# Moving the third mixer's implicit filter and its transform to the start of a one-core, three-block Trainium2 kernel

## Chip, cores and metric

The kernel is one launch on one core of a Trainium2 chip. The metric is device time in microseconds (us) of that core; the time before is the median of 3 runs.

## What is computed

A two-layer diffusion-style block runs over 256 latent and 256 context rows of width 1024. A third block follows on 16 meta tokens and the 256 latent rows. Its mixer has a long convolution whose filter does not depend on the data that flows through the kernel: it comes from three small weight matrices, two sines and a decay. Cut to what matters here:

```python
def hyena_filter(L, w1, b1, w2, b2, w3, b3, freq):          # L = 272, D_HY = 512
    z = concatenate([t, cos(bands * w), -sin(bands * w)])    # constants, (272, 33)
    hdn = sin(freq[0] * (z @ w1 + b1))                       # (272, 64)
    hdn = sin(freq[1] * (hdn @ w2 + b2))
    k = (hdn @ w3 + b3).reshape(L, 2, D_HY) * exp(-t * deltas)
    return concatenate([k_fwd, zeros, k_bwd[:0:-1]])

def fft_long_conv(u, k_full, skip):                          # y = irfft(rfft(u) * rfft(k_full))[:L] + u * skip

def second_block(x, meta, ...):                              # the third mixer
    proj = rmsnorm(h) @ w_in
    y_hy = hyena_branch(proj[..., :s_hy], ...)               # short conv, fft_long_conv, projection
    y_rg = rglru_branch(...)                                 # two directions of conv, gates, scan
    merged = sigmoid(gates) * y_hy + sigmoid(gates) * y_rg
```

## The kernel before

All engines have their instructions written out by hand; the order on each queue is the order of the text. SyncE streams weight blocks of 512 KB into a ring of six places; a place is loaded again when its last block has begun (for unsplit blocks) or has been split. Most weight blocks are split by ScalarE (`high`, line 1575) and VectorE (`low`, line 1969) into a high and a low part, and TensorE does three products for each of eight chunks of 128 inputs.

The stages that matter here:

- **Start.** TensorE takes 16 modulation blocks `ada0a` (line 728). Behind block 7 stands `norm(0)`, the sum of squares of the input rows (line 767), behind block 11 the spread of the factor (line 782). `first_turn` (line 752) turns the modulation; ScalarE (line 1493) and VectorE make the split input chunk by chunk; the first projection tile of `ev_in` (line 939) takes each chunk as it comes, and nine tiles follow, the last five with a 128x512 product for the squares of queries and keys (line 834). Meanwhile VectorE has a chain of small steps at the very start (`softplus`, lines 1962 to 1969).
- **`fourier`.** Before its first product (line 819) TensorE takes eight modulation blocks.
- **Third mixer.** `mix` (line 1134) makes 44 projection tiles. Among them, on TensorE: `rg_gates(0)` and `rg_gates(1)` (line 1077), two small products for the filter's hidden layers (lines 1184 and 1187), six tap products (line 1195), and, between tiles 37 and 38, the filter's transform (`filter_dft`, line 1090: 18 fp32 products into five groups). VectorE makes the sine arguments (seven steps each), multiplies the taps by the decay (`filt`) and adds and subtracts them, between the `low` parts and the steps of the recurrent branch (`rg_conv`, `rg_logs`, `rg_ratio`, `rg_scan`). ScalarE does the two sines (with their table loads), the copies of the transform (`dft_copy`, line 1734) and the recurrent branch's functions; `mults(1)` (line 1726, a square root of 128x2176) stands behind three of the copies.
- On VectorE the three parts of `rg_scan(1, ...)` (lines 2301, 1969, 2308) stand ahead of `low_mix(40)`, so TensorE's tile 40 needs the scan.
- The filter's weights, the decay (1536 KB) and the transform's table (960 KB) are loaded by GpSimd just before the third mixer.

Of the kernel before, what the change touches and what calls it, by code (L numbers as in the profile page):

```python
# [14 lines left out]
F32 = mybir.dt.float32  # L15
F32R = mybir.dt.float32r
# [109 lines left out]
for _n, _c in PARAMS:  # L126
# [19 lines left out]
MASKO0 = 41984  # L146
# [6 lines left out]
PARTA0, PARTB0, PARTC0 = 30608, 38144, 42496  # L153
SQB0 = 14144
XC0, RG0, IG0, TG0, HFW0 = (14144 + 2176 * _i for _i in range(5))
FILT0 = 25024
HID0 = 26448
KF0 = 27536
KS0 = 32768
FCOS0 = 35840  # L160
# [13 lines left out]
RGATE0 = 25024  # L174
MT0 = 14144
# [19 lines left out]
SMALLS = [("ident", 128), ("ones", 128), ("block", 128), ("perm", 128), ("iota", 128), ("iota16", 16),  # L195
          ("pick", 12), ("strip", 4), ("eps", 1)]
# [55 lines left out]
def build(nc, t, out):  # L252
    with ExitStack() as ctx:
# [48 lines left out]
        with nc.sbuf_tensor("mixer_rows_place", [P, NP0], F32):  # L302
            with nc.sbuf_tensor("n0_parts", [P, 2 * DC * LT], F32R) as n0_parts:
                with nc.sbuf_tensor("mixer_gates_place", [P, PARTA0 - NP0 - 2 * DC * LT], F32):
                    with nc.sbuf_tensor("mix_w_parts0", [P, 2048], F32R) as mix_w_parts0:
                        with nc.sbuf_tensor("filter_place", [P, PARTB0 - PARTA0 - 2048], F32):
                            with nc.sbuf_tensor("mix_w_parts2", [P, 2048], F32R) as mix_w_parts2:
                                with nc.sbuf_tensor("residual_rows_place", [P, PARTC0 - PARTB0 - 2048], F32):
                                    with nc.sbuf_tensor("mix_w_parts1", [P, 2048], F32R) as mix_w_parts1:
                                        pass  # L310
# [13 lines left out]
        query_parts = {name: [[first, query_w_parts1, mix_w_parts1][(r - turn) % PARTS][:, :].rearrange("p (h n) -> p h n", h=2)  # L324
                              for r in range(PARTS)] for name, first in (("wq", query_w_parts0), ("peer0", ahead_w_parts0))}
        n0p = n0_parts[:, :].rearrange("p (h c n) -> p h c n", h=2, c=DC)
# [50 lines left out]
        ident, ones, block64, perm, iota = (small(n) for n in ("ident", "ones", "block", "perm", "iota"))  # L377

# [7 lines left out]
        hyena_in = sem("hyena_tables_in")  # L386
# [55 lines left out]
        pool_chain = sem("pool_chain")  # L442
        hres_ready = sem("second_residual_ready")
# [14 lines left out]
        bias_row = sem("filter_bias_row_ready")  # L458
# [3 lines left out]
        filt_sums = sem("filter_sums_ready")  # L462
# [120 lines left out]
        mask_o = view(MASKO0, QT, L)  # L583
# [82 lines left out]
        def _(pe):  # L666
# [118 lines left out]

            def fourier():
# [3 lines left out]
                for f in fill[0][:8]:  # L790
                    ada(*f)
                pe.wait_ge(even_in, 16 * 4)
# [266 lines left out]
            z = view(FILT0, LT, parts=EMB)  # L1059
            w1 = view(FILT0 + LT, HF, parts=EMB)  # L1060
            w2 = view(FILT0 + LT + HF, HF, parts=HF)
            w3 = view(FILT0 + LT + 2 * HF, 2 * HY, parts=HF + 1)
            hid = view(HID0, 4, LT)
            ktab, ks = view(FCOS0, 3, GW), view(KS0, 2, 3, HY)

# [15 lines left out]

            def filter_dft(g):

                if g >= 2:
                    pe.wait_ge(dft_copied, g - 1)
                o = bank[4 + g % 2]
                runs = [(0, P, g // 2)] if g < 4 else [(0, 64, 0), (64, P, 1)]
                for tt in range(3):
                    for lo, hi, src in runs:
                        mm = pe.matmul(o[lo:hi, :], ktab[0:TTW[tt], tt, g * P + lo:g * P + hi],  # L1090
                                       ks[0:TTW[tt], src, tt, :], start=(tt == 0), stop=(tt == 2))
                mm.then_inc(dft_ready, 1)
# [17 lines left out]
            def mix_first():  # L1110

                wb = [split_block(ORD["w_in2a"] + j, None, mwp) for j in range(2)]
                o = [bank_of(TILE["w_in2a"] + j) for j in range(2)]
                for k in range(DC):
                    pe.wait_ge(normed, DC * 4 + k + 1)
                    for j in range(2):
                        for n, (hw, hx) in enumerate(TERMS):
                            mm = pe.matmul(o[j][:, 0:LT], wb[j][:, hw, k, :], n0p[:, hx, k, :],
# [64 lines left out]
            pe.wait_ge(hyena_in, 16 * 6)  # L1183
            pe.matmul(bank[3][0:HF, 0:LT], w1, z, start=True, stop=True).then_inc(hid_ready, 1)
            mix(16, 24)
            pe.wait_ge(hid_sin, 1)
            pe.matmul(bank[4][0:HF, 0:LT], w2, hid[0:HF, 0, :], start=True, stop=True).then_inc(hid_ready, 1)
            mix(24, 28)
            pe.wait_ge(hid_sin, 2)
            pe.wait_ge(bias_row, 1)  # L1190
            for n in range(6):
                tt = n // 2
                if n >= 2:
                    pe.wait_ge(filt_read, n - 1)
# [6 lines left out]
            for g in range(GROUPS):  # L1201
                filter_dft(g)
# [1889 lines left out]
```

## Time and profile before

| | |
|---|---|
| median of 3 runs | 2191.51 us (2190.57 to 2192.89) |
| the profiled execution's own time | 2190.52 us |
| its span, first to last instruction | 2188.6 us |
| TensorE busy | 96% of the span |
| VectorE, ScalarE, GpSimd busy | 65%, 44%, 14% |
| mean granted TensorE clock | 0.988 |

The timeline has one row for a run of equal instructions: start and length in us, engine, line, operation, tiles written and read, count, and in brackets the idle time before it with what ended it. An fp32 product shows as two records of TensorE. PEld is TensorE's weight load. The page has shares by engine; the windows give busy time of each engine and the granted clock in a stretch.

### The profile page before, as it was taken

How to read it: one execution, taken by the hardware profiler on the slowest of the kernel's cores; microseconds unless marked ns; L12 is line 12 of the kernel's file. 1: busy time of each engine (PE TensorE's matmuls, PEld its weight loads, DVE VectorE, ACT ScalarE, POOL GpSimd, SP SyncE). 2: the span in 40 equal slices, each digit the busy share in tenths (PEclk: the TensorE clock that was granted, in tenths of full speed). 3: DMA queues.
4: the chain of work that ended last, by engine and by line, in shares of the span. 5: the costliest groups of instructions: out<-in, count | busy, mean ns of one | idle time of the engine just before them, and what ended most of it. 6: DMA issues, size and time to landing. Idle time of an engine off the chain costs nothing.

```text
span 2188.6 us, 35310 instructions
## 1 busy us (share of the span) xinstructions
PE 2102.2 (96%) x12873; PEld 1777.8 (81%) x12873; DVE 1432.7 (65%) x2494; ACT 972.8 (44%) x1532; POOL 315.3 (14%) x336
## 2 busy tenths in 40 slices
PE   6999999999989998999999999999999999999998
PEld 2745788888878747999998788999988888888886
DVE  4436544443258585665569776997996677777776
ACT  3335322222244365444476725546753444444444
POOL 0014000000013030000000004787840000000000
PEclk8999999999999999999999999999999999999999
DMA  8266222222235264455644434452146555555553
GB/s 319 78 228 244 87 96 96 96 96 96 96 93 162 87 248 167 164 182 184 208 157 143 171 122 155 165 183 78 68 144 221 180 195 190 187 188 191 188 188 124
DMA packets 92847, 342.90 MB, mean 157 GB/s; under 512 B 10393, under 2 KB 10420, under 8 KB 92224
## 3 DMA queue, kind: packets, MB, share of 16 engines
q1 hardware_dynamic: 89280, 325.10, 43.9%
q0 software_dynamic: 3456, 16.26, 2.4%
q8 instruction: 76, 1.25, 0.2%
q14 instruction: 35, 0.29, 0.0%
HBM read 340.27 MB, written 1.05 MB: 156 GB/s over the span
## 4 chain that ended last, share of the span: by engine, by line
PE 60%; issue 27%; DVE 8%; ACT 3%; DMA 2%; POOL 0%; SPq 0%; DVEq 0%; ACTq 0%; POOLq 0%
PE banks L939 20%; PE banks L986 8%; PE banks L1281 6%; PE banks L1134 3%; PE banks L1330 3%; PE banks L864 2%; PE banks L1314 2%; PE banks L1018 2%; DVE main_zone L1966 2%; PE banks L1403 1%; PE banks L728 1%; PE banks L890 1%; PE banks L953 1%; PE banks L911 1%; DVE main_zone L1969 1%
## 5 line engine op out<-in xcount | busy, mean ns | idle before, releaser
L939 PE MATMUL banks<-act_parts,first_w_parts 128*128 128x512 f32 (+1 forms) x2592 | 477.5, 345 | 6.0 <-DVE act_parts L1969 3.9
L939 PEld LDWEIGHTS banks<-act_parts,first_w_parts 128*128 128x128 f32 x2592 | 410.8, 190 | 69.6 <-issue 7.6
L1969 DVE TENSOR_TENSOR first_w_parts<-weight_ring,first_w_parts 128x1024 fp32r<-128x1024 f32 x166 | 206.8, 1248 | 258.6 <-ACT first_w_parts L1575 258.6
L1403 PE MATMUL banks<-w_parts,a_parts 128*128 128x512 f32 x1524 | 360.1, 390 | 0.6 <-DVE a_parts L1969 0.6
L1403 PEld LDWEIGHTS banks<-w_parts,a_parts 128*128 128x128 f32 x1524 | 285.9, 188 | 59.6 <-DVE a_parts L1969 1.0
L1969 DVE TENSOR_TENSOR w_parts<-weight_ring,w_parts 128x1024 fp32r<-128x1024 f32 x207 | 254.4, 1230 | 72.1 <-ACT w_parts L1575 72.0
L1575 ACT ACTIVATE w_parts<-weight_ring 128x1024 fp32r<-128x1024 f32 x207 | 218.9, 1058 | 184.2 <-PE banks L1369 102.0
L1575 ACT ACTIVATE first_w_parts<-weight_ring 128x1024 fp32r<-128x1024 f32 x166 | 174.7, 1057 | 232.5 <-PE banks L939 120.6
L1369 PE MATMUL banks<-n_parts,w_parts 128*128 128x512 f32 x632 | 229.4, 397 | 1.3 <-DVE w_parts L1969 1.3
L986 PE MATMUL banks<-ffn_hidden_parts,first_w_parts 128*128 128x512 f32 (+1 forms) x1056 | 183.4, 336 | 0.0
L986 PEld LDWEIGHTS banks<-ffn_hidden_parts,first_w_parts 128*128 128x128 f32 x1056 | 162.5, 190 | 20.6
L1372 PE MATMUL banks<-n_parts,w_parts 128*128 128x256 f32 x632 | 164.4, 281 | 0.0
L1369 PEld LDWEIGHTS banks<-n_parts,w_parts 128*128 128x128 f32 x632 | 118.6, 188 | 26.8 <-DVE w_parts L1969 1.7
L1134 PEld LDWEIGHTS banks<-n_parts,mix_w_parts 128*128 128x128 f32 x1008 | 123.7, 188 | 11.9 <-DVE mix_w_parts L1969 8.8
L1134 PE MATMUL banks<-n_parts,mix_w_parts 128*128 128x256 f32 (+1 forms) x1008 | 127.9, 287 | 5.2 <-DVE mix_w_parts L1969 5.2
L1969 DVE TENSOR_TENSOR banks<-banks,main_zone 128x256 f32<-128x256 f32 (+1 forms) x174 | 97.7, 566 | 53.2 <-ACT main_zone L1893 52.5
L1372 PEld LDWEIGHTS banks<-n_parts,w_parts 128*128 128x128 f32 x632 | 119.5, 189 | 6.1
L1969 DVE TENSOR_TENSOR mix_w_parts<-weight_ring,mix_w_parts 128x1024 fp32r<-128x1024 f32 x60 | 72.9, 1222 | 33.9 <-ACT mix_w_parts L1575 33.3
L1575 ACT ACTIVATE mix_w_parts<-weight_ring 128x1024 fp32r<-128x1024 f32 x77 | 81.0, 1053 | 16.4 <-PE banks L1134 7.9
L1893 ACT ACTIVATE main_zone<-banks 128x256 f32<-128x256 f32 x79 | 30.3, 384 | 124.3 <-PE banks L1369 124.3
L728 PE MATMUL banks<-weight_ring,small_zone 128*32 128x512 f32 x384 | 62.4, 641 | 18.6 <-DMA weight_ring<-in_stream 10.0
L2902 POOL DMA_DIRECT2D main_zone<-in_g_final x1 | 0.6, 616 | 538.9 <-DVE a_parts L1969 538.9
(296 smaller groups left out, 3055.8 us busy)
## 6 DMA issues: line engine op xcount, KB each, us to landing
weight_ring<-in_stream SPq DMA_DIRECT2D x618, 512.0 KB, 3.8
main_zone<-in_rel_bias POOLq DMA_DIRECT2D x6, 512.0 KB, 12.3
rounded<-in_dft_input POOLq DMA_DIRECT2D x1, 1600.0 KB, 7.0
main_zone<-in_decay POOLq DMA_DIRECT2D x1, 1536.0 KB, 9.4
rounded<-in_dft_inverse POOLq DMA_DIRECT2D x1, 1280.0 KB, 6.2
main_zone<-in_xT POOLq DMA_DIRECT2D x1, 1024.0 KB, 11.6
main_zone<-in_ctxT POOLq DMA_DIRECT2D x1, 1024.0 KB, 16.1
tail_zone<-in_rel_bias POOLq DMA_DIRECT2D x2, 512.0 KB, 24.1
```

The costliest lines, as they stand in the source:

```text
L728: mm = pe.matmul(bank[ADA_BANKS[phase][half]][strip:strip + 32, :], cond[:, k, 10 - 2 * row:42 - 2 * row], wb[:, half * 512:(half + 1) * 512],
L864: mm = pe.matmul(bank[b][:, :], fin[:, hx, c, tt * P:(tt + 1) * P], wb[:, hw, kk, :], start=(c == 0 and n == 0), stop=(c == DC - 1 and n = ...
L939: mm = pe.matmul(o[:, 0:w], wb[:, hw, k, :], fin[:, hx, k, 0:w], start=(k == 0 and n == 0), stop=(k == DC - 1 and n == 2))
L986: mm = pe.matmul(o[:, 0:w], wb[:, hw, b % 8, :], fhid[:, hx, k, 0:w], start=(k == 0 and n == 0), stop=(k == FC - 1 and n == 2))
L1134: mm = pe.matmul(o[:, cols], wb[:, hw, k, :], n0p[:, hx, k, cols], start=(k == 0 and n == 0), stop=(k == DC - 1 and n == 2))
L1281: mm = pe.matmul(o[:, 0:L], wb[:, hw, k, :], rows[:, hx, k, :], start=(k == 0 and n == 0), stop=(k == DC - 1 and n == 2))
L1330: mm = pe.matmul(twins[h][:, j * P:(j + 1) * P], one1[:, 8 * h + j, :], one2[:, 8 * h + j, :], start=True, stop=True)
L1369: return pe.matmul(o[:, :], w[:, 0, k, :], n2p[:, :, k, :], start=(k == 0), stop=(k == DC - 1))
L1372: return pe.matmul(o[:, 0:L], w[:, 1, k, :], n2p[:, 0, k, :], start=False, stop=False)
L1403: mm = pe.matmul(acc[n][:, :], ap_[:, e % 3, ha, (n // 2) * P:(n // 2 + 1) * P], wp[(B + b) % PARTS][:, hw, (n % 2) * 512:(n % 2 + 1) * 51 ...
L1575: act.activation(parts[n % PARTS][:, 0, :], slot(s), ACT.Copy).then_inc(w_hi, 1)
L1969: return dve.tensor_tensor(o, a, b, op)
```

## The change

The filter is made at the start. The first small product stands behind modulation block 2, the second behind block 4; the tap products 0 and 1 behind block 7, ahead of `norm(0)`; the others behind blocks 8 to 11. The sum and the difference of the two halves of the last weight matrix are made by VectorE before the products, so that the taps need no sums afterwards; GpSimd mends the first tap. The decay is made by ScalarE with 12 exponentials instead of being loaded. Of the transform, groups 0, 1 and 2 (nine products) go into and behind the first `ev_in` tile, groups 3 and 4 among the eight modulation blocks ahead of `fourier`. ScalarE copies the spectrum at these places (`dft_copy(0)` stands ahead of the last chunk of the split input). The spectrum stays in columns that are free until the third mixer; GpSimd moves the last group once. On the loads: the filter's first weights come ahead of the input rows, its last weights behind them, the transform's table when modulation block 14 begins, the rest of the small constants behind it, and the tables of `fourier` only after the first tile. The places of two split buffers move, the first block of the third mixer is split into another buffer, and the odd mask is 64 columns wide.

The core of the diff:

```diff
-SMALLS = [("ident", 128), ("ones", 128), ("block", 128), ...
+SMALLS = [("ones", 128), ("iota", 128), ("pick", 12), ("strip", 4), ("eps", 1), ("fade", 15),
+          ("ident", 128), ("block", 128), ("perm", 128), ("iota16", 16)]
+NEARLY = 288
...
+            def tap_product(n):
+                tt, src = n // 2, n % 2
+                if n == 0:
+                    pe.wait_ge(hid_sin, 2)
+                    pe.wait_ge(taps_w, 1)
+                if n >= 2:
+                    pe.wait_ge(filt_read, n - 1)
+                pe.matmul(bank[2 + n % 2][0:TTW[tt], :], hid[0:HF + 1, 2, tt * P:tt * P + TTW[tt]], w3_both[:, src, :],
+                          start=True, stop=True).then_inc(filt_ready, 1)
+            def filter_dft(g, steps=range(3)):
+                if 0 in steps:
+                    if g == 0:
+                        pe.wait_ge(ktab_in, 16)
+                        pe.wait_ge(filt_read, 6)
+                        pe.wait_ge(filt_fixed, 2)
+                    if g >= 2:
+                        pe.wait_ge(dft_copied, [1, 3, 4][g - 2])
...
+            def first_tile():
...
+                    if k >= 1:
+                        filter_dft((k - 1) // 3, [(k - 1) % 3])
+                filter_dft(2, [1, 2])
             def fourier():
-                for f in fill[0][:8]:
+                pe.wait_ge(dft_copied, 2)
+                for f in fill[0][:6]:
                     ada(*f)
+                filter_dft(3)
+                ada(*fill[0][6])
+                filter_dft(4)
+                ada(*fill[0][7])
+                pe.wait_ge(dft_copied, GROUPS)
...
             for b in range(16):
                 ada(0, "ada0a", b, b // DC, b // DC == 0, b // DC == 1)
+                if b in (2, 4):
+                    hidden(b // 2 - 1)
                 if b == 7:
+                    tap_product(0)
+                    tap_product(1)
                     norm(0)
+                if 8 <= b < 12:
+                    tap_product(b - 6)
                 if b == 11:
                     spread_rstd(0)
             first_turn()
-            for j in range(10):
-                split_tile("ev_in", j, T, k_norm=0 if j == 0 else None)
+            first_tile()
+            pe.wait_ge(tables_in, 16)
+            for j in range(1, 10):
+                split_tile("ev_in", j, T)
...
             rg_gates(0)
-            pe.wait_ge(hyena_in, 16 * 6)
...
+            mix(16, 34)
             rg_gates(1)
             mix(34, 38)
-            pe.wait_ge(filt_sums, 1)
-            for g in range(GROUPS):
-                filter_dft(g)
             mix(38, 44)
...
 ScalarE:
                 for c in range(DC):
+                    if k == 0 and c == DC - 1:
+                        dft_copy(0)
...
+            for tt in range(3):
+                for b in range(4):
+                    act.activation(decay[:, tt, b * P:(b + 1) * P], iota, ACT.Exp, ...
+            sine(0)
+            sine(1)
             norm(0)
...
             decays(1, lambda: split2(36, 38))
-            for g in range(3):
-                dft_copy(g)
             mults(1)
-            for g in range(3, GROUPS):
-                dft_copy(g)
...
 VectorE:
-            softplus()
+            softplus(0)
+            sine_arg(0)
+            dve.memset(hid[HF:HF + 1, 2, :], 1.0)
+            sine_arg(1)
+            softplus(1)
+            dve.wait_ge(taps_w_in, 16)
+            tt_(w3_both[:, 0, :], w3[:, 0, :], w3[:, 1, :], ALU.add)
+            tt_(w3_both[:, 1, :], w3[:, 0, :], w3[:, 1, :], ALU.subtract).then_inc(taps_w, 1)
+            filt(0)
+            filt(1)
             first_norm()
...
 GpSimd:
+            pool.dma_start(view(HYZ0, LT + 2 * HF, parts=HF), t["hyena_first"][:, :]).then_inc(hidden_in, 16)
             pool.dma_start(X[:, :, 0:L], ...
             pool.dma_start(X[:, :, L:T], ...
+            pool.dma_start(view(HYW0, 2 * HY, parts=HF + 1), t["hy_w3"][:, :]).then_inc(taps_w_in, 16)
...
+            pool.wait_ge(blocks_used, 15)
+            pool.dma_start(ktab, t["dft_filter"].rearrange("p (a n) -> p a n", a=3)).then_inc(ktab_in, 16)
             pool.wait_ge(ada_rows, 1)
+            pool.dma_start(view(SMALL0 + NEARLY, NSM - NEARLY), t["smalls"][:, NEARLY:NSM]).then_inc(tables_in, 16)
+            pool.wait_ge(tile_ready, TILE["ev_in"] + 1)
             pool.dma_start(view(DFTE0, 1280), t["dft_even"][:, :]).then_inc(even_in, 16)
```

How the instructions move, at the three places on which the prediction rests. First TensorE from its first modulation block on, before the change (small_zone holds constants, main_zone the input rows and work):

```order
L728 MATMUL banks<-weight_ring,small_zone 32x512 x16
L767 MATMUL banks<-main_zone,small_zone 32x128 x32
L728 MATMUL banks<-weight_ring,small_zone 32x512 x8
L782 MATMUL banks<-small_zone 128x128 x4
L728 MATMUL banks<-weight_ring,small_zone 32x512 x8
```

The same place now (L801 and L804 are the two hidden products, L814 the taps, L778 the sum of squares):

```order
L739 MATMUL banks<-weight_ring,small_zone 32x512 x6
L801 MATMUL banks<-main_zone 64x272
L739 MATMUL banks<-weight_ring,small_zone 32x512 x4
L804 MATMUL banks<-main_zone 64x272
L739 MATMUL banks<-weight_ring,small_zone 32x512 x6
L814 MATMUL banks<-main_zone 128x512 x2
L778 MATMUL banks<-main_zone,small_zone 32x128 x32
```

Four filter products now stand ahead of the sum of squares on TensorE.

Second, the end of the first `ev_in` tile on TensorE now (L842 are the tile's products, L830 the transform's, L1011 the next tiles):

```order
L842 MATMUL banks<-act_parts,first_w_parts 128x512 x3
L830 MATMUL banks<-tail_zone,main_zone 128x512
L842 MATMUL banks<-act_parts,first_w_parts 128x512 x3
L830 MATMUL banks<-main_zone 128x512
L830 MATMUL banks<-tail_zone,main_zone 128x512 x2
L1011 MATMUL banks<-act_parts,first_w_parts 128x512 x120
```

Before, the tile's 24 products and the next tiles' 120 were one unbroken run of 144 (L939).

Third, ScalarE in the third mixer behind the second direction's gates, before the change (L1720 and L1722 are the decay's exponential and square, L1734 the copies of the transform, L1726 the square root, L1575 the split of block 40):

```order
L1720 ACT_TABLE_LOAD
L1720 ACTIVATE main_zone<-main_zone 128x2176
L1722 ACTIVATE main_zone<-main_zone 128x2176
L1734 ACTIVATE main_zone<-banks 128x512 x3
L1726 ACT_TABLE_LOAD
L1726 ACTIVATE main_zone<-main_zone 128x2176
L1734 ACTIVATE main_zone<-banks 128x512 x2
L1575 ACTIVATE mix_w_parts<-weight_ring 128x1024
```

And now:

```order
L1795 ACT_TABLE_LOAD
L1795 ACTIVATE main_zone<-main_zone 128x2176
L1797 ACTIVATE main_zone<-main_zone 128x2176
L1801 ACT_TABLE_LOAD
L1801 ACTIVATE main_zone<-main_zone 128x2176
L1627 ACTIVATE mix_w_parts<-weight_ring 128x1024
```

The five copies are gone from between the square, the square root and the next split.

## Rows read from the trace of the kernel before

**Rows 1.** Timeline, 0 to 70 us: start, length, engine, line, operation, tiles, count.
```profile
10.05 0.18 DVE L1962 TENSOR_SCALAR small_zone<-small_zone 128x16 f32<-128x16 f32 x1 [1.27 <-ACT small_zone L1638]
...
14.40 1.05 PE L728 MATMUL banks<-weight_ring,small_zone 128*32 128x512 f32 x4 [1.01 <-DMA weight_ring<-in_stream]
14.57 0.18 DVE L1966 SCALAR_TENSOR_TENSOR small_zone<-small_zone 128x16 f32<-128x16 f32 x1
...
23.21 2.01 PE L767 MATMUL banks<-main_zone,small_zone 128*32 128x128 f32 x64 [0.28 <-ACT main_zone L1466]
...
31.70 1.05 PE L728 MATMUL banks<-weight_ring,small_zone 128*32 128x512 f32 x4 [0.73 <-DMA weight_ring<-in_stream]
...
41.94 5.46 PE L939 MATMUL banks<-act_parts,first_w_parts 128*128 128x512 f32 x12 [2.72 <-DVE act_parts L1969]
...
52.19 0.60 ACT L1514 ACTIVATE main_zone<-banks 128x512 f32<-128x512 f32 x1 [4.78 <-PE banks L939]
```
**Rows 2.** Windows: stretch, its length, busy PE, PEld, DVE, ACT, POOL; PEclk, DMA share, GB/s.
```profile
40.00:42.00 2.00, 0.06 (x1) 0.09 (x1) 2.00 (x6) 2.00 (x6) 0.00 (x0) 0.50 1.01 397
...
48.00:50.00 2.00, 1.72 (x6) 0.95 (x6) 2.00 (x6) 0.00 (x0) 0.00 (x0) 1.00 0.65 229
...
1071.00:1080.00 9.00, 8.92 (x59) 8.95 (x60) 6.28 (x15) 5.02 (x10) 0.88 (x2) 0.81 0.99 378
```
**Rows 3.** Timeline, the pace of `ev_in` tiles without and with a 128x512 product.
```profile
57.65 0.60 ACT L1514 ACTIVATE main_zone<-banks 128x512 f32<-128x512 f32 x1 [3.92 <-PE banks L939]
...
85.58 1.02 PE L834 MATMUL banks<-main_zone,small_zone 128*128 128x512 f32 x2
...
91.93 1.02 PE L834 MATMUL banks<-main_zone,small_zone 128*128 128x512 f32 x2
```
**Rows 4.** Timeline, TensorE ahead of `fourier`.
```profile
105.58 2.78 PE L728 MATMUL banks<-weight_ring,small_zone 128*32 128x512 f32 x24
...
110.18 1.05 PE L728 MATMUL banks<-weight_ring,small_zone 128*32 128x512 f32 x4 [1.81 <-DMA weight_ring<-in_stream]
...
114.30 2.59 PE L819 MATMUL banks<-main_zone 128*128 128x256 f32 x8
```
**Rows 5.** Timeline, TensorE in the third mixer.
```profile
1128.06 0.67 PE L1184 MATMUL banks<-main_zone 33*64 33x272 f32 x2
...
1167.08 1.02 PE L1195 MATMUL banks<-main_zone 65*128 65x512 f32 x2
...
1170.77 1.02 PE L1195 MATMUL banks<-main_zone 65*128 65x512 f32 x2
...
1210.10 5.89 PE L1090 MATMUL banks<-tail_zone 128*128 128x512 f32 x12
1216.68 8.87 PE L1090 MATMUL banks<-tail_zone 128*128 128x512 f32 x24 [0.69 <-ACT main_zone L1734]
1225.49 5.95 PE L1134 MATMUL banks<-n_parts,mix_w_parts 128*128 128x256 f32 x48
1232.66 3.11 PE L1134 MATMUL banks<-n_parts,mix_w_parts 128*128 128x256 f32 x24 [1.22 <-DVE mix_w_parts L1969]
```
**Rows 6.** Timeline, VectorE and ScalarE in the third mixer.
```profile
1135.60 0.55 DVE L1963 TENSOR_SCALAR main_zone<-banks,small_zone 64x272 f32<-64x272 f32 x1
...
1138.24 0.29 DVE L1963 TENSOR_SCALAR main_zone<-main_zone 64x272 f32<-64x272 f32 x1
...
1173.68 0.68 DVE L1969 TENSOR_TENSOR main_zone<-banks,main_zone 128x512 f32<-128x512 f32 x1
...
1216.18 2.43 DVE L1966 SCALAR_TENSOR_TENSOR main_zone<-main_zone 128x2176 f32<-128x2176 f32 x1 [5.62 <-ACT main_zone L1722]
...
1221.66 2.02 ACT L1726 ACTIVATE main_zone<-main_zone 128x2176 f32<-128x2176 f32 x1
```
**Rows 7.** DMA issues: transfer, queue, count, size, median us from issue to landing.
```profile
tail_zone<-in_dft_filter POOLq DMA_DIRECT2D x1, 960.0 KB, 5.0
main_zone<-in_mask_even POOLq DMA_DIRECT2D x1, 512.0 KB, 9.1
```

More of the change, by code:

```diff
@@ new lines, in filter_dft @@
+            def filter_dft(g, steps=range(3)):
[6 more added lines that the diff above has]
+                        pe.wait_ge(dft_copied, [1, 3, 4][g - 2])
+                o = bank[DFT_BANKS[g]]
+                runs = [(0, P, g // 2)] if g < 4 else [(0, 64, 0), (64, P, 1)]
+                for tt in steps:
+                    for lo, hi, src in runs:
+                        mm = pe.matmul(o[lo:hi, :], ktab[0:TTW[tt], tt, g * P + lo:g * P + hi],
+                                       taps[src][tt][0:TTW[tt]], start=(tt == 0), stop=(tt == 2))
+                if 2 in steps:
+                    mm.then_inc(dft_ready, 1)
@@ new lines, in first_tile @@
+            def first_tile():
+                wb = split_block(ORD["ev_in"])
+                o = bank_of(TILE["ev_in"])
+                for k in range(DC):
+                    pe.wait_ge(normed, k + 1)
+                    for n, (hw, hx) in enumerate(TERMS):
+                        mm = pe.matmul(o[:, :], wb[:, hw, k, :], fin[:, hx, k, :],
+                                       start=(k == 0 and n == 0), stop=(k == DC - 1 and n == 2))
+                        if k == 0 and n == 0:
+                            mm.then_inc(parts_begun, 1)
+                    if k == DC - 1:
+                        mm.then_inc(tile_ready, 1)
+                    if k >= 1:
+                        filter_dft((k - 1) // 3, [(k - 1) % 3])
+                filter_dft(2, [1, 2])
@@ L1080, in rg_gates @@
                     mm.then_inc(tile_ready, 1)
[L1082 to L1092, printed above, removed]
             def input_dft(i):
@@ L1110, in mix_first @@
             def mix_first():
-                wb = [split_block(ORD["w_in2a"] + j, None, mwp) for j in range(2)]
+                pe.wait_ge(w_lo, ORD["w_in2a"] + 1)
+                second = split_block(ORD["w_in2a"] + 1, None, mwp)
                 o = [bank_of(TILE["w_in2a"] + j) for j in range(2)]
@@ L1506, in project_in @@
                     high(name, PARTS - 1)
+                    dft_copy(1)
+                if l == 0 and j == 1:
+                    dft_copy(2)
                 b = tile(name, j)
@@ L1644, in _ @@
             qk_root(0, 4)
+            dft_copy(3)
+            dft_copy(4)
             for u in range(9):
@@ L1985, in first_norm @@
                 dve.reciprocal(rstd[:, 0:w], rstd[:, 0:w]).then_inc(rstd_ready, 1)
+                for n in range(2, 6):
+                    filt(n)
                 dve.wait_ge(rstd_spread, 1)
@@ L2947, in tables @@
     ok = (cq[None] >= c0[:, None]) & (cq[None] < c0[:, None] + 16)
-    mask_odd = np.tile(np.where(ok, 0, NEG).astype(f), (2, 8))
+    mask_odd = np.tile(np.where(ok, 0, NEG).astype(f), (2, 1))
     N = 2 * FQ
```

231 lines of the change are left out of this document (111 added, 120 removed).

## The prediction

> **What bounds the kernel now.** I read the page's chain first: TensorE carries it, so a change counts where it delays or relieves TensorE, or what TensorE waits for. Then the timeline of the two places that the change joins.
>
> At the start [rows 1] TensorE is not full. Modulation blocks come one by one from the ring (the rows at 14.40 and 31.70 end a wait for a transfer), the sum of squares runs at 23.21, the first `ev_in` tile begins at 41.94, and its copy at 52.19 says that the tile is done about 0.3 us earlier, at 51.9. The reader is to see a tile of 10.0 us where the next takes 57.65 - 52.19 = 5.5 [rows 1, 3]: it is held by VectorE and ScalarE, and partly runs at the lower clock level (granted 0.50, that is 1.2 GHz, at 40 to 42 us, and 1.00 at 48 to 50) [rows 2].
>
> In the third mixer [rows 5] TensorE is nearly unbroken, and the filter's products stand in its line: the transform alone from 1210.10 to 1225.49, 15.4 us. But two tiles later, at 1232.66, TensorE waits for VectorE. This is the row that decides most: weight block 40 is split only behind the second scan, and the scan hangs on the square root on ScalarE at 1221.66 [rows 6].
>
> **The change, part by part.** All against the profiled execution's own 2190.5 us (span 2188.6, the rest around it is not touched); the median of the runs is 1.0 above it.
>
> *Third mixer up to the second gates: -5.6.* Gone from TensorE are two hidden products of about 0.65 (the row at 1128.06) [rows 5], 1.3, and six tap products. From tap to tap are 1170.77 - 1167.08 = 3.69, and a tile alone takes 5.95 / 2 = 2.97, so a tap costs 0.72 and six 4.3. VectorE follows: it sheds in the same stretch two sine arguments of 1138.24 + 0.29 - 1135.60 = 2.93 and six multiplications of 0.68 [rows 6], 9.9 in all, more than TensorE, so it does not hold the gates back. Bounds 4 and 7.
>
> *From the second gates to tile 40: -3.0 of 15.4.* The transform's 15.4 us leave TensorE, but its next wait does not leave. The chain gates, logs, tanh, exponential, square, ratio, square root, scan, split of block 40 runs on ScalarE and VectorE and holds nothing of the transform but the copies ahead of the square root. The ratio is done at 1216.18 + 2.43 = 1218.61; the square root begins at 1221.66, kept back by the third copy, whose product came late, and by the table load behind it [rows 6]. Without the copies the load lies ahead of the ratio's end and the root can follow it: 3.0 earlier. So tile 40 begins 5.6 + 3.0 = 8.6 earlier, and TensorE, which is through tile 39 another 15.4 - 3.0 + 1.2 = 13.6 sooner, waits these 13.6. What is late next is the same scan as before. Bounds 2 and 15.4.
>
> *The clock behind that wait: +0.7.* After a stretch in which TensorE mostly waited for a norm, the granted clock of the next 9 us was 0.81 (from 1071) [rows 2], so part of them was at the lower level. Tile 40 may then take up to twice its 2.97, but the tiles there are paced by the splits, so most is made up. Bounds 0 and 3. The Trainium skill ("TensorE: Matmul & The Clock Gate", Part 1) says that an idle engine falls back to 1.2 GHz; by it, tile 40 runs wholly at that level, about 3.0 more at its own end; the trace agrees in that such a stretch is seen behind a wait.
>
> *Start, ahead of the sum of squares: +2.9.* TensorE's queue is in order, so the sum of squares (23.21) now waits for tap products 0 and 1, and these for a chain: modulation block 4 ends at 15.45 [rows 1], hidden product 0.67, sine argument 2.93 to 19.1, then on VectorE what is left of `softplus` (10.05 to 14.75 before: 4.7) to 23.8, the two weight sums at 0.68 as a 128x512 step [rows 6] to 25.1, two taps of 0.5 to 0.7 with a sine long done: 26.1 instead of 23.2. Blocks 8 and later follow, the ring's next loads hang on their beginning, so the modulation ends later by the same. The other four taps lie among these blocks and are covered by the wait for transfers. Bounds 1 (only the two taps) and 5 (12 exponentials and a table load on ScalarE ahead of the first sine).
>
> *The table on the way: +0.5.* GpSimd asks for 960 KB when block 14 begins (31.70 + 2.9 = 34.6); such a load took 5.0 in the third mixer, a load half its size beside the ring 9.1 [rows 7]. The first transform step comes after two chunks of the tile, about 47.5. It should be there, but the second `ev_in` block shares the way. Bounds 0 and 4.
>
> *First `ev_in` tile: +6.2.* Nine products of 128x512 fp32 go into and behind it. One such product between tiles of the same stage costs (91.93 - 85.58) - 5.46 = 0.9 [rows 3]; a row of the transform itself says 5.89 / 6 = 0.98, a tap 0.72 [rows 5]. The tile's 24 own products take 5.46 at the full level, 0.68 a chunk. I let the low level last as long as now, 5.2 us: it holds chunks 0 and 1 (2.7), one transform step (1.8) and half a chunk. Left are 5.5 chunks (3.75) and eight steps (7.2): 41.94 + 16.15 = 58.1 instead of 51.9. VectorE's pace, which set it before, is now hidden. Bounds 4.6 (at 0.72) and 9.4 (at 0.98, and a low level that lasts some 2.5 us more).
>
> *Ahead of `fourier`: +1.7.* Six blocks end at 108.36 [rows 4]; group 3, three products, fills the wait until block 6 (110.18) and passes it, 111.1; block 6 at the pace of the six, 0.46, ends at 111.5; group 4 waits for the copy of group 3, 112.2, and takes 8.87 - 3 x 0.98 = 5.9 less another three, 2.95 [rows 5]: 115.1; block 7 and the last copy, 116.0, instead of 114.3. Bounds 0 and 3.
>
> The rest costs nothing: the wider row of GpSimd's mask addition and the move of the last group lie far ahead of their readers, the tables of `fourier` have 50 us, and the two moved split buffers keep their order.
>
> Sum: 2.9 + 0.5 + 6.2 + 1.7 = +11.3 at the start, -8.6 + 0.7 = -7.9 in the mixer: **+3.4**. Own time 2193.9, from the median 2194.9; I take 2194. About 0.2%, 4.4 us, is what a measurement of this kernel can tell from no change.
>
> **The rivals.**
>
> *A. The transfer decides (slower), chance 0.21.* The table of 960 KB shares the engines with modulation block 15 and the first `ev_in` blocks. At 397 GB/s [rows 2] it is 2.5 us of all engines. ScalarE splits `ev_in` blocks 0 and 1 ahead of the 16 pieces of the split input, so a late block delays every chunk. It decides as soon as block 1 or the table lands after its reader; at the row of 9.1 for 512 KB, 960 KB take up to 17, 34.6 + 17 = 51.6, 4 after its step. Price 4 there and up to 2 in the blocks: with the forecast's +3.4 some +8, 2199. The Trainium skill ("DMA: Bandwidth & Descriptors", Queues, rings and completion order) says that an engine takes turns between the queues that have work; by it the ring gets only half of the way while the table runs, which is this rival. No run here shows the table beside the ring at the start.
>
> *B. The start covers it, chance 0.10.* The transform steps fall into the tile's slack of 4.5 us (10.0 against 5.5), the taps into waits for transfers: the start costs 5, the sum is 5 - 7.9 = -2.9, 2187.6. Against it: more than half of that slack is the lower clock level (24 products at half rate take 10.9), which does not go away.
>
> *C. The scan does not hold, chance 0.07.* If tile 40 came with the rest, the mixer would give 5.6 + 15.4 = 21.0: 2190.5 + 11.3 - 21.0 = 2180.8. Against it stands the wait at 1232.66, which is there already with the transform in front of it.
>
> **How the numbers follow.** The forecast has 0.62; with its bounds it spans 2190 to 2198, of which about 0.17 lies past 2195.9 and the rest within 0.2%. Rival A adds 0.21 to slower. B gives 0.07 to same and 0.03 to faster, C 0.07 to faster. Faster 0.10, same 0.52, slower 0.38. The range reaches down into B and up to A, 2188 to 2200, and leaves out C and A's tail.
>
> **What would show it.** Right: the sum of squares near 26, the first tile ending 15 to 18 us after its beginning, `fourier` about 11 us later than now; in the mixer no filter products, and a wait of some 13 us of TensorE for VectorE ahead of tile 40. Wrong: TensorE waiting for a transfer ahead of the first transform step (A); no such wait at tile 40 (C); a first tile of about 11 us (B).

## Result and the profile after

The changed kernel takes 2201.73 us (median of 5 runs, 2200.61 to 2204.60) where the kernel before takes 2191.51 beside it (5 runs, 2187.22 to 2192.89): a ratio of 1.0043, 95% interval 1.0032 to 1.0054. It is slower, and outside the range of the forecast. The profiled execution is the slowest of the five, 2204.60 with a span of 2202.7, 14.1 above the span of before. Between the medians it is 10.2: this execution is 2.9 above its median, and the profiled one of before 1.0 below its own.

Following TensorE through both traces shows where the kernel falls behind and where it catches up:

| TensorE begins | before | after | later by |
|---|---|---|---|
| sum of squares, `norm(0)` | 23.21 | 30.13 | 6.9 |
| modulation block 8 | 25.05 | 33.55 | 8.5 |
| first `ev_in` tile | 41.94 | 51.81 | 9.9 |
| first product of `fourier` | 114.30 | 132.18 | 17.9 |
| sum of squares behind the first attention | 257.42 | 273.29 | 15.9 |
| sum of squares ahead of `od_in` | 626.59 | 644.11 | 17.5 |
| scores of the second attention | 765.25 | 786.27 | 21.0 |
| third mixer, first gates | 1119.41 | 1140.31 | 20.9 |
| second gates | 1191.40 | 1206.41 | 15.0 |
| tile 40 | 1232.66 | 1244.67 | 12.0 |
| first output tile of the mixer | 1246.82 | 1259.89 | 13.1 |

**The start.** The timeline of the changed kernel answers to [rows 1]:

```profile
17.22 1.16 PE L804 MATMUL banks<-main_zone 64*64 64x272 f32 x2 [0.32 <-ACT main_zone L1705]
...
21.29 0.16 DVE L2021 TENSOR_SCALAR small_zone<-small_zone 128x16 f32<-128x16 f32 x1
...
23.44 1.78 PE L739 MATMUL banks<-weight_ring,small_zone 128*32 128x512 f32 x4 [0.47 <-DMA weight_ring<-in_stream]
...
25.96 1.29 DVE L2028 TENSOR_TENSOR main_zone<-main_zone 65x512 f32<-65x512 f32 x2
...
27.40 2.81 PE L814 MATMUL banks<-main_zone 65*128 65x512 f32 x4 [2.18 <-DVE main_zone L2028]
...
30.13 3.64 PE L778 MATMUL banks<-main_zone,small_zone 128*32 128x128 f32 x64
...
33.55 1.84 PE L739 MATMUL banks<-weight_ring,small_zone 128*32 128x512 f32 x4
...
44.40 0.65 POOL L2857 DMA_DIRECT2D main_zone<-in_dft_filter  x1 [10.82 <-PE banks L739]
...
51.81 2.90 PE L842 MATMUL banks<-act_parts,first_w_parts 128*128 128x512 f32 x6 [4.08 <-DVE act_parts L2028]
```

The second hidden product (17.22) waits for the first sine, `softplus` runs from 21.29 to the weight sums at 25.96, and TensorE waits for these sums ahead of taps 0 and 1 (27.40). Behind that wait taps and sum of squares run slowly: the sum of squares takes 33.55 - 30.13 = 3.4 to block 8, where before it took 1.8. The windows (stretch, length, busy PE, PEld, DVE, ACT, POOL; granted clock, DMA share, GB/s) say why, and what else stands still:

```profile
26.00:28.00 2.00, 0.60 (x2) 0.40 (x3) 1.25 (x2) 0.64 (x1) 0.00 (x0) 1.00 1.01 397
28.00:30.00 2.00, 2.00 (x4) 0.39 (x2) 0.69 (x1) 0.00 (x0) 0.00 (x0) 0.59 0.31 125
30.00:32.00 2.00, 2.00 (x37) 1.74 (x40) 0.69 (x1) 0.00 (x0) 0.98 (x1) 0.50 0.00 0
32.00:34.00 2.00, 2.00 (x38) 1.59 (x32) 0.00 (x0) 0.16 (x1) 1.48 (x3) 0.50 0.03 8
34.00:36.00 2.00, 2.00 (x6) 0.30 (x2) 0.95 (x1) 0.21 (x1) 0.00 (x0) 0.70 0.00 0
```

TensorE was busy for 0.60 of the 2 us ahead of 28; from 28 on the clock was granted at 0.59 and 0.50 (0.50 is 1.2 GHz). That wait is not the only one: block 7 (23.44), behind a wait for its transfer, already took 1.78 where a block takes 1.05 at the full level [rows 1]. The transfers stop as well: the DMA share falls to 0.31 and then 0.00. TensorE begins no block from 23.44 to 33.55, and while it begins none, no place of the ring comes free.

**First tile and `fourier`.** TensorE's timeline; these rows answer to [rows 3, 4]:

```profile
54.51 1.60 PE L830 MATMUL banks<-main_zone 128*128 128x512 f32 x2
55.43 1.36 PE L842 MATMUL banks<-act_parts,first_w_parts 128*128 128x512 f32 x3
...
66.06 2.07 PE L830 MATMUL banks<-tail_zone,main_zone 128*128 128x512 f32 x4
68.06 7.33 PE L1011 MATMUL banks<-act_parts,first_w_parts 128*128 128x512 f32 x31
```

```profile
121.66 2.78 PE L739 MATMUL banks<-weight_ring,small_zone 128*32 128x512 f32 x24
...
132.18 1.99 PE L891 MATMUL banks<-main_zone 128*128 128x256 f32 x8
```

The tile with its nine transform steps takes 68.06 - 51.81 = 16.25. No step waits for the table: asked for at 44.40 and landed 9.5 later, at 53.9, it is there 0.6 ahead of the first step (54.51).

**`od_in`.** The offset grows by 3.5 between 644 and 786 us, far from any edit to TensorE. All engines at that place:

```profile
704.01 5.63 DVE L2028 TENSOR_TENSOR first_w_parts<-weight_ring,first_w_parts 128x1024 fp32r<-128x1024 f32 x1
...
709.57 3.34 DVE L2142 RECIPROCAL main_zone<-main_zone 128x512 f32<-128x512 f32 x1
...
714.07 4.97 POOL L2903 TENSOR_TENSOR tail_zone<-tail_zone,small_zone 128x2048 f32<-128x2048 f32 x1
714.58 5.54 DVE L2028 TENSOR_TENSOR first_w_parts<-weight_ring,first_w_parts 128x1024 fp32r<-128x1024 f32 x1
...
720.17 4.15 PE L1011 MATMUL banks<-act_parts,first_w_parts 128*128 128x512 f32 x11 [3.88 <-DVE first_w_parts L2028]
```

A split that elsewhere takes 1.22 takes 5.6 beside GpSimd's mask addition and ends 1.1 behind the addition's end (714.07 + 4.97 = 719.04; 714.58 + 5.54 = 720.12). TensorE waits 3.88 for it.

**Third mixer.** All engines; the rows answer to [rows 5, 6], the windows below them to [rows 2]:

```profile
1206.41 7.58 PE L1151 MATMUL banks<-main_zone,weight_ring 128*128 128x136 f32 x64
1213.73 17.16 PE L1198 MATMUL banks<-n_parts,mix_w_parts 128*128 128x256 f32 x144
...
1231.22 2.43 DVE L2025 SCALAR_TENSOR_TENSOR main_zone<-main_zone 128x2176 f32<-128x2176 f32 x1 [5.63 <-ACT main_zone L1797]
1233.68 2.02 ACT L1801 ACTIVATE main_zone<-main_zone 128x2176 f32<-128x2176 f32 x1 [1.19 <-DVE main_zone L2025]
...
1244.67 11.31 PE L1198 MATMUL banks<-n_parts,mix_w_parts 128*128 128x256 f32 x72 [13.78 <-DVE mix_w_parts L2028]
1256.94 3.10 PE L1198 MATMUL banks<-n_parts,mix_w_parts 128*128 128x256 f32 x24 [0.96 <-DVE mix_w_parts L2028]
```

```profile
1244.00:1248.00 4.00, 3.33 (x15) 3.33 (x16) 3.97 (x3) 2.83 (x6) 0.00 (x0) 0.50 0.40 131
1248.00:1252.00 4.00, 4.00 (x27) 4.00 (x26) 3.64 (x3) 1.80 (x3) 0.00 (x0) 0.71 0.42 135
```

The transform's rows are gone. The square root follows the ratio at once, and TensorE waits 13.78 at tile 40; behind that wait the clock is 0.50.

### The profile page after: what moved, and what is told of

The parts are those of the page before. It is cut to its first block, busy times and chain, and to the rows that moved or that the text cites. A ratio compares the mean times of both kernels' runs of the same rounds, so it can differ in the third digit from the quotient of the medians.

```text
span 2202.7 us, 35323 instructions
## 1 busy us (share of the span) xinstructions
PE 2106.8 (96%) x12873; PEld 1781.4 (81%) x12873; DVE 1434.8 (65%) x2490; ACT 975.8 (44%) x1543; POOL 318.1 (14%) x338
## 3 DMA queue, kind: packets, MB, share of 16 engines
q8 instruction: 76, 1.25, 0.2%
HBM read 338.52 MB, written 1.05 MB: 154 GB/s over the span
## 4 chain that ended last, share of the span: by engine, by line
PE 62%; issue 26%; DVE 8%; ACT 3%; DMA 1%; POOL 0%; DVEq 0%; ACTq 0%; POOLq 0%; SPq 0%
PE banks L1011 20%; PE banks L1058 8%; PE banks L1328 6%; PE banks L1198 4%; PE banks L1377 3%; PE banks L936 2%; PE banks L1361 2%; DVE main_zone L2025 2%; PE banks L1098 2%; PE banks L739 2%; PE banks L1450 1%; PE banks L962 1%; PE banks L983 1%; PE banks L971 1%; PE banks L1025 1%
## 5 line engine op out<-in xcount | busy, mean ns | idle before, releaser
L1011 PE MATMUL banks<-act_parts,first_w_parts 128*128 128x512 f32 (+1 forms) x2568 | 469.6, 344 | 5.0 <-DVE first_w_parts L2028 4.1
L1011 PEld LDWEIGHTS banks<-act_parts,first_w_parts 128*128 128x128 f32 x2568 | 405.8, 190 | 66.8 <-DVE first_w_parts L2028 6.0
L1328 PE MATMUL banks<-n_parts,query_w_parts 128*128 128x256 f32 x888 | 109.9, 284 | 1.9 <-POOL query_w_parts L2923 1.9
L1328 PEld LDWEIGHTS banks<-n_parts,query_w_parts 128*128 128x128 f32 x888 | 107.7, 192 | 2.4 <-POOL query_w_parts L2923 2.3
L2923 POOL TENSOR_TENSOR query_w_parts<-weight_ring,query_w_parts 128x1024 fp32r<-128x1024 f32 x41 | 99.0, 2419 | 51.1 <-ACT query_w_parts L1627 31.3
```

The lines of the kernel that those rows point to most:

```text
L1011: mm = pe.matmul(o[:, 0:w], wb[:, hw, k, :], fin[:, hx, k, 0:w], start=(k == 0 and n == 0), stop=(k == DC - 1 and n == 2))
L1328: mm = pe.matmul(o[:, 0:L], wb[:, hw, k, :], rows[:, hx, k, :], start=(k == 0 and n == 0), stop=(k == DC - 1 and n == 2))
L2923: pool.tensor_tensor(w[:, 1, :], slot(s), w[:, 0, :].bitcast(F32), ALU.subtract).then_inc(w_lo, 1)
```

## Experiments

Ratios are to the kernel before, run in the same comparison (its medians were 2191.51 to 2192.80). "In its trace" means TensorE's offset to the profile of before.

**1. Without the filter at the start.** All of the filter's work is left out; its spectrum is set to zero.

```diff
-                if b in (2, 4):
-                    hidden(b // 2 - 1)
...
-                    if k >= 1:
-                        filter_dft((k - 1) // 3, [(k - 1) % 3])
...
+            for o in kspec + [last_early]:
+                dve.memset(o, 0.0).then_inc(dft_copied, 1)
```

> Leaves the filter and its transform out altogether (its spectrum is set to zero by five short memsets on VectorE in an idle stretch), so only what the third mixer gives is left. If the mixer gives what the two profiles show between its first gates and the output tiles (5.9 + 3.0 - 1.1 = 7.8), the time is 2191.5 - 7.8 = 2183.7, about 0.9964 of before. If it gives only what is left in the changed kernel (end +14.1 against +17.3 at the start, some 3.5), 2188.0.

2183.32 us, ratio 0.9954 (0.9941 to 0.9967). In its trace the kernel is 3.8 late at the first gates and 4.2 early at the output tiles, a gain of 8.0 in the mixer; TensorE's rows:

```profile
1189.28 7.58 PE L1138 MATMUL banks<-main_zone,weight_ring 128*128 128x136 f32 x64
...
1227.54 11.05 PE L1185 MATMUL banks<-n_parts,mix_w_parts 128*128 128x256 f32 x72 [13.78 <-DVE mix_w_parts L2001]
```

So the mixer gives what it should, and what makes the changed kernel slow lies outside it. The 3.8 are not shown to be a cost: this execution took 2187.20, 3.9 above the median of its five. The later loads of the constants and of the tables of `fourier`, the odd mask of 64 columns and the moved buffers are all still in this kernel; its median leaves no price for them. The 3.5 at `od_in` do not appear here (3.7 late ahead of it, 3.6 behind it), although two splits took 5.62 and 5.61 beside the same additions: they fell so that TensorE waited only 1.23. All engines:

```profile
698.26 5.06 POOL L2859 TENSOR_TENSOR tail_zone<-tail_zone,small_zone 128x2048 f32<-128x2048 f32 x1
698.78 5.61 DVE L2001 TENSOR_TENSOR first_w_parts<-weight_ring,first_w_parts 128x1024 fp32r<-128x1024 f32 x1
...
704.45 5.72 PE L1004 MATMUL banks<-act_parts,first_w_parts 128*128 128x512 f32 x24 [1.23 <-DVE first_w_parts L2001]
```

**2. `softplus` later.** Its fourteen tiny steps move behind the query and key norms.

```diff
             sine_arg(1)
-            softplus(1)
...
             qk_norm(0)
+            softplus(1)
```

> Only the fourteen tiny softplus steps (4.64 us) move from ahead of the weight sums to behind the query and key norms of the first layer. Theory (the chain on VectorE holds the sum of squares): taps 0 and 1 directly behind block 7 (25.3), the sum of squares near 26.5 instead of 30.13 and at the higher clock level, block 8 near 28.5 instead of 33.55, first ev_in tile near 47 instead of 51.81: about 5 faster than the changed kernel, 2196.7. Rival (the ring is late by itself): the sum of squares moves, the first tile by 1 at most, 2200.7.

2202.64, ratio 1.0041 (1.0028 to 1.0054): no gain that can be told from none. The theory of a chain on VectorE alone falls. All engines:

```profile
23.03 1.29 DVE L2028 TENSOR_TENSOR main_zone<-main_zone 65x512 f32<-65x512 f32 x2 [2.41 <-DMA main_zone<-in_hy_w]
...
23.32 1.92 PE L739 MATMUL banks<-weight_ring,small_zone 128*32 128x512 f32 x4 [0.86 <-DMA weight_ring<-in_stream]
...
25.17 3.78 PE L814 MATMUL banks<-main_zone 65*128 65x512 f32 x4
...
28.88 3.64 PE L778 MATMUL banks<-main_zone,small_zone 128*32 128x128 f32 x64
```

The weight sums now wait for the load of the last weight matrix. The taps stand directly behind block 7 (25.17), without a wait, but at the lower level they take 3.7, so the sum of squares comes at 28.88, only 1.25 earlier, and takes 3.4 again. The level was low already at block 7 (1.92 at 23.32), behind waits for transfers, and was granted at 0.50 from 20 to 32: it does not need the wait for the weight sums. The first tile is 2.4 earlier.

**3. Sum of squares first.** Only the order on TensorE changes, and VectorE's order with it.

```diff
                 if b == 7:
-                    tap_product(0)
-                    tap_product(1)
                     norm(0)
-                if 8 <= b < 12:
-                    tap_product(b - 6)
+                if b == 9:
+                    tap_product(0)
+                    tap_product(1)
+                if 10 <= b < 14:
+                    tap_product(b - 8)
```

> Only the order: the sum of squares goes ahead of the taps, taps 0 and 1 behind block 9, the others behind blocks 10 to 13; the weight sums still wait for softplus. Theory (TensorE's queue waits for the taps): sum of squares near 25.4, block 8 near 27.4, the taps beside the transfers; first tile near 46 to 47: about 5 to 6 faster than the changed kernel, 2196. Rival (ring): 1 faster at most, 2200.7. Rival (the taps cost the same wherever they stand): 2 to 3 faster, 2199.

2198.67, ratio 1.0024 (1.0015 to 1.0033), 4 us less than the changed kernel by the ratios. That lies between the theory (2196) and the rival by which the taps cost the same wherever they stand (2199), and the times alone do not choose. The trace does. TensorE, then the windows of the stretch that stood still:

```profile
25.13 3.27 PE L778 MATMUL banks<-main_zone,small_zone 128*32 128x128 f32 x64
28.14 1.12 PE L739 MATMUL banks<-weight_ring,small_zone 128*32 128x512 f32 x8
29.19 1.98 PE L814 MATMUL banks<-main_zone 65*128 65x512 f32 x4
...
46.39 2.90 PE L842 MATMUL banks<-act_parts,first_w_parts 128*128 128x512 f32 x6 [4.00 <-DVE act_parts L2029]
```

```profile
30.00:32.00 2.00, 2.00 (x7) 0.33 (x5) 1.38 (x2) 0.00 (x0) 0.01 (x1) 1.00 0.80 250
32.00:34.00 2.00, 2.00 (x8) 0.44 (x6) 0.69 (x1) 0.00 (x0) 1.90 (x3) 1.00 1.01 358
```

Block 8 begins at 28.14 in place of 33.55 and the first tile at 46.39 in place of 51.81, 5.4 earlier each; the DMA share at 30 to 34 is 0.80 and 1.01 where it was 0.00 and 0.03, the granted clock 1.00 where it was 0.50. At `fourier` 4.8 of the 5.4 are left. This is the term that failed: the place of the taps ahead of the sum of squares, with the blocks and so the ring queued behind it. The sum of squares itself is slow here too (28.14 - 25.13 = 3.0, 1.8 before).

**4. Both edits of 2 and 3.**

> Both edits of the two runs beside it. If either alone takes TensorE's wait away, both together give no more than the better of them within 1 us: 2196. If softplus also held the taps among the blocks, 1 to 2 more: 2194.5.

2197.75, ratio 1.0019 (1.0010 to 1.0028): within 1 us of experiment 3, as expected; `softplus` costs nothing once the taps stand elsewhere.

**5. Mask additions in pieces.** GpSimd's four additions of 128x2048 become 32 of 128x256.

```diff
-                    b = view(BIAS0 + (2 * qt + g) * 8 * L, 8 * L // 64, 64)
-                    last = pool.tensor_tensor(b, b, mask_o.unsqueeze(1).broadcast_to([P, 8 * L // 64, 64]), ALU.add)
+                    for n in range(8):
+                        b = view(BIAS0 + (2 * qt + g) * 8 * L + 256 * n, 4, 64)
+                        last = pool.tensor_tensor(b, b, mask_o.unsqueeze(1).broadcast_to([P, 4, 64]), ALU.add)
```

> GpSimd's four mask additions of 128x2048 become 32 of 128x256, nothing else. Theory: while one of them runs, an operation of VectorE on two tensors waits for its end (5.6 us instead of 1.22 for a split in the changed kernel, at 704 and 715 us), and TensorE then waits 3.88 us for the split; small pieces take that wait away: 3 to 5 faster than the changed kernel, 2197 to 2199, and no split of od_in over 2 us. Rival (the wait at 720 us comes from the late landing of the bias tables or from the ring): no change, 2201.7. If the pieces cost GpSimd more than they save, the odd attention begins later: slower than 2201.7.

2198.18, ratio 1.0030 (1.0018 to 1.0041), 2.8 less by the ratios, whose intervals overlap; the trace is clearer. All engines:

```profile
698.82 20.75 POOL L2904 TENSOR_TENSOR main_zone<-main_zone,small_zone 128x256 f32<-128x256 f32 x24 [28.66 <-DMA tail_zone<-in_rel_bias]
...
709.53 1.76 DVE L2028 TENSOR_TENSOR first_w_parts<-weight_ring,first_w_parts 128x1024 fp32r<-128x1024 f32 x1
...
715.05 6.03 PE L1011 MATMUL banks<-act_parts,first_w_parts 128*128 128x512 f32 x24
```

No split takes over 1.76, and TensorE waits for none. The offset falls from 17.4 ahead of `od_in` to 14.6 at the first gates, where the changed kernel's rises from 17.5 to 20.9. The Trainium skill ("SBUF — State Buffer", section "SBUF: two separate sides") says that VectorE and GpSimd share one pair of ports, that an operation of VectorE with two inputs in that memory may need it, and that the later of the two waits for the other's whole instruction. The trace agrees: the split (two inputs) went from 1.22 to 5.6, the reciprocal (one input) beside the same additions stayed at 3.34 (709.57).

**6. The same on the kernel before.**

```diff
-                    last = pool.tensor_tensor(bias[qt][g], bias[qt][g],
-                                              mask_o[:, qt, :].unsqueeze(1).broadcast_to([P, 8, L]), ALU.add)
+                    for n in range(8):
+                        last = pool.tensor_tensor(bias[qt][g][:, n, :], bias[qt][g][:, n, :], mask_o[:, qt, :], ALU.add)
```

> The kernel before, with GpSimd's four mask additions in 32 pieces and nothing else. Theory: in the kernel before one split also takes 5.6 us behind a mask addition, but TensorE waits only 1.26 and 0.38 for it, so this gives 1 to 2: 2190.5 to 2191.5 where before is 2192.7. If it gives as much as on the changed kernel (2.8 by the ratios), the additions cost both kernels alike and are no part of the difference: 2189.9.

2189.95, ratio 0.9990 (0.9980 to 1.0000), 2.2 less by the ratio. By the times the pieces thus give both kernels about as much (2.8 and 2.2), which is what was expected if the additions are no part of the difference; the intervals are too wide to tell. The traces do tell: over `od_in` the pieces give 2.6 here and 6.3 in the changed kernel. In before one split fell on the additions (5.60 at 688.70) and TensorE waited 1.26 for it. In all seven traces with the filter at the start and whole additions `od_in` costs 3.1 to 3.8 more than before; the bias table that lands last takes 29.0 to 29.7 from issue to landing in these seven, 27.5 before and 27.8 in experiment 1, and the additions begin behind it. Why it lands later was not tried and stays open.

**7. Block 40 split ahead of the scan.**

```diff
             decays(1, lambda: split2(36, 38))
+            high_mix(40)
             mults(1)
...
             rg_ratio(1)
+            low_mix(40)
             for part in range(3):
                 rg_scan(1, part)
-            low_mix(40)
```

> In the third mixer weight block 40 is split ahead of the second scan (ScalarE's half ahead of the square root, VectorE's between ratio and scan), nothing else. Theory (behind the scan VectorE's own chain sets the output tiles; TensorE's wait of 13.8 us only shows it): tile 40 begins near 1235 in place of 1244.7, the first output tile only 1.2 earlier, one split less on the chain: 2200.5. Rival (the scan's hold on TensorE is the loss): the whole wait comes back, some 10 faster, 2191.7.

2201.49, ratio 1.0035 (1.0022 to 1.0047): by the ratios 1.7 less, intervals overlapping. TensorE and its waits:

```profile
1234.33 5.41 PE L1198 MATMUL banks<-n_parts,mix_w_parts 128*128 128x256 f32 x24 [3.94 <-DVE mix_w_parts L2028]
...
1246.63 7.32 PE L1198 MATMUL banks<-n_parts,mix_w_parts 128*128 128x256 f32 x48 [6.90 <-DVE mix_w_parts L2028]
```

Tile 40 comes 10.3 earlier, yet the first output tile follows the second gates by only 2.2 less than in the changed kernel (1.2 expected). TensorE's 13.8 is not a price: behind the scan VectorE's own chain sets the pace, and the wait only moves to tile 41.

**8. Three transform steps twice.** The spectrum then counts the middle taps twice.

```diff
+                        for again in range(2 if tt == 1 and g < 3 else 1):
-                        mm = pe.matmul(o[lo:hi, :], ktab[0:TTW[tt], tt, g * P + lo:g * P + hi],
+                            mm = pe.matmul(o[lo:hi, :], ktab[0:TTW[tt], tt, g * P + lo:g * P + hi],
```

> Three of the nine transform steps in the first ev_in tile are issued twice (the middle step of each of three groups, so the spectrum counts the middle taps twice); it prices a step there. Theory (TensorE carries the tile): 3 x 0.98 = 2.9 slower than the changed kernel, 2204.6. Rival (the steps lie in the tile's slack beside VectorE and ScalarE): no change within 0.5, 2201.7.

2206.89, ratio 1.0057 (1.0044 to 1.0070), 3.1 more by the ratios. In its trace the tile goes from 51.94 to 70.76, 18.82 in place of 16.25: 0.86 a step. The steps are paid in full.

**9. TensorE kept busy ahead of the first tile.** Four products that nobody reads.

```diff
             first_turn()
+            for n in range(4):
+                pe.matmul(bank[6][:, :], ones, X[:, n, 0:T], start=True, stop=True)
```

> On the changed kernel, four 128x512 products whose result nobody reads fill TensorE's wait of 4.1 us ahead of the first ev_in tile. Theory (that wait is what drops the granted clock to 0.50 at 50 to 54 us, and the drop costs the tile two chunks and a step at half rate): granted 1.00 through the tile, the tile 16.25 - 2.3 = 14 us, 2199.4. Rival (the first chunks are paced by VectorE at 1.25 us anyway): the clock stays up, the tile is 1 shorter at most, 2200.7. If the four products outlast the wait, up to 0.5 slower than either.

2202.45, ratio 1.0044 (1.0030 to 1.0057): nothing. Windows of its trace:

```profile
48.00:52.00 4.00, 4.00 (x13) 2.11 (x13) 3.86 (x12) 3.89 (x8) 0.00 (x0) 0.64 1.01 398
52.00:56.00 4.00, 4.00 (x14) 2.28 (x12) 4.00 (x11) 4.00 (x9) 0.00 (x0) 0.94 1.01 398
```

The tile shrinks from 16.25 to 14.76 (53.50 to 68.26). But the fillers themselves ran partly at the lower level (0.64 at 48 to 52) and lasted up to the tile's beginning, longer than the wait that they were to fill, so that from the turn to the tile TensorE needed 6.62 in place of 6.02. That leaves 0.9 gained, nearer the rival's 1 than the theory's 2.3.

**10. Together.** Experiments 2, 3, 5 and 7 on the changed kernel; then with the fillers of 9; and before with 6 and 9.

> softplus late, sum of squares first, mask additions in pieces and block 40 ahead, all on the changed kernel. If the terms add: 2197.75 (the two edits at the start) - 3 to 5 - 1.2 = 2191.5 to 2193.5, level with the kernel before. If the mask pieces or block 40 bring nothing, 2196.5 to 2197.7.

> All edits that helped on the changed kernel (softplus late, sum of squares first, mask additions in pieces, block 40 ahead) and the four filling products. If these keep the first tile at the higher level also here: 2195.2 - 2.3 = 2192.9, level with before; if the chunks are paced by VectorE, 2194.5.

> The kernel before with the mask additions in pieces and the filling products. Its first tile (24 products in 10.0 us, five of them at granted 0.50) is paced by VectorE and ScalarE at 1.25 a chunk, so a higher clock gives it 0 to 1: 2189.5 to 2191.5.

2195.17 (ratio 1.0010, 0.9999 to 1.0022), 2192.19 (1.0003, 0.9993 to 1.0012) and 2191.33 (0.9994, 0.9985 to 1.0003). The repaired change is level with the kernel before, not ahead of it. Of the kernels that compute the whole result, the lowest is before with the pieces (experiment 6), and its interval touches 1. The first of the three fell some 2.6 short of its parts, added by the ratios. In its trace the end of the second attention ran at the lower level (TensorE):

```profile
842.96 1.97 PE L983 MATMUL banks<-tail_zone,main_zone 128*64 128x128 f32 x16 [0.69 <-ACT tail_zone L1617]
...
850.21 4.93 PE L1125 MATMUL banks<-act_parts 128*128 128x256 f32 x24 [0.72 <-DVE act_parts L2029]
```

The same rows take 1.09 and 3.14 in the changed kernel, with like waits ahead of them (0.75, 0.72). Between the scores of the second attention and the mixer's first gates this trace loses 5.2 to before, where that of the changed kernel loses nothing. One execution shows it, not more.

## Why the prediction was wrong

The direction of each part was right and most sizes too; the forecast failed on one step of the start. The traces add a contention that it left out.

- **"Start, ahead of the sum of squares: +2.9"** is the step that failed. Block 8, which "follows", came 8.5 later. Of the miss, 2.1 is the chain: the weight sums ended at 27.25, not 25.1, because the second hidden product waited for the first sine (17.22, not 15.45), which the chain had left out, and took 1.16, not 0.67. 1.7 is the two taps, 2.7 instead of 1.0, and 1.6 the sum of squares itself, 3.4 instead of 1.8: both run mostly at the lower level. That is not the price of TensorE's wait of 2.18 alone, since in experiment 2, without it, they took 3.7 and 3.4. I had seen that falling clock in [rows 2] and priced it in the mixer and the first tile, but not here. The bound of 5 did not hold it either. Experiment 3 takes the taps away from there, and 5.4 come back in the trace, 4 in the time.
- **"The other four taps ... are covered by the wait for transfers"** did not hold: with the ring idle from 30 to 36 and its blocks at hand there was no such wait left to cover them. Between block 8 and the first tile another 1.4 was lost, where 0.5 stood for the table.
- **"First `ev_in` tile: +6.2"** was right in its mechanism, 0.86 a step in experiment 8, and in its sum, 16.25 for 16.15, but there with some luck: two chunks and one step at the lower level took 55.43 - 51.81 = 3.6 for the 4.5 reckoned, and what followed 68.06 - 55.43 = 12.6 for 11.65.
- **"Ahead of `fourier`: +1.7"** was right: from six blocks to the first product 132.18 - 121.66 = 10.5, before 8.7, +1.8.
- **The mixer, -7.9**, was right in all its parts: up to the second gates 20.9 - 15.0 = 5.9 (5.6), to tile 40 another 3.0 (3.0), the clock behind the wait 13.1 - 12.0 = 1.1 (0.7). Experiment 1 gives 8.0 without the start. That most of the transform's 15.4 us would turn into a wait at tile 40 was the reading that mattered most, and it held: 13.78 measured, 13.6 worked out.
- **"The rest costs nothing: the wider row of GpSimd's mask addition ..."** was right of the row: the four additions take 14.89 + 4.97 = 19.9 and 19.5 before, and experiment 1 has the same row without a loss. What the forecast left out is whom an addition holds up while it runs, and that it can fall on another split once the transfers shift against the tiles: 3.5 in the trace. The times of experiments 5 and 6 leave open whether it is part of the difference.
- **Rival A** named a time near the result, for another reason. The table landed before its step, and the stretch from the turn to the first tile grew from 5.65 to 6.02 only. **Rival B** is excluded by the tile, **rival C** by the wait at tile 40.

With 17.9 for 11.3 at the start the forecast of +3.4 becomes 3.4 + 6.6 = 10.0, against 10.2 between the medians; with the 3.5 at `od_in` it is 13.5, against 14.1 between the profiled executions. The start alone thus accounts for the miss of the medians, and how much of `od_in` is in them stays open.

## What to carry to other kernels

Work that is small by its durations is dear when it is put ahead of something that a whole queue follows: here two taps of 1 us each, and the chain that they waited for, held up the weight loads behind them, and TensorE passed most of them at half its clock. Before moving work into a stretch that seems to have slack, ask what paces the stretch; slack of a transfer-paced queue is gone as soon as the consumer stops. And a wait that grows on a busy engine is not yet a gain to be had: follow the chain that ends it.

## What was not expected of the hardware

- An operation of VectorE on two tensors ended just behind a whole GpSimd instruction: it took 5.63 and 5.54 us in place of 1.22, and 1.76 with GpSimd's work in eighths. The pieces cost GpSimd more in all, 0.86 each (20.75 / 24), 27.7 for 32 against 14.89 + 4.97 = 19.9, in time that nothing waited for.
- From 28 to 36 the windows of the changed kernel were granted at 0.50 to 0.70, though TensorE was busy throughout them. Ahead of them stood waits of 0.80 and 0.47 for transfers and of 2.18 for VectorE. Experiment 2 had no wait for VectorE there, and its taps and sum of squares were as slow.
- The price of the same overlap hangs on where it falls: splits of 5.6 us beside the additions cost TensorE waits of 1.26 before, 1.23 in experiment 1 and 3.88 in the changed kernel.
